# Second mixer: keys in columns with the meta keys as side columns, both kinds of values in one row stream

## The reference

```
hn   = rms_norm(h) * gain                    # h: 16 meta tokens and 256 tokens
proj = hn @ w_in                             # 1024 -> 1824 columns
c_q, c_kv, k_rope, dq, dk, dv, sq, sk, sv = split(proj)
#  256   128    32     256 256 256 384 128 128
y_a = mla(c_q, c_kv, k_rope)                 # 6 heads, through small second projections
y_b = differential(dq, dk, dv)               # 4 heads, two softmaxes each, 32 wide
y_c = sliding_window(sq, sk, sv, sinks)      # 6 heads, 2 key heads, 64 wide
h   = h + concat(y_a, y_b, y_c) @ w_out
```

## Time and profile before

| | us |
|---|---|
| median of 3 runs | 1275.91 (1275.83 to 1276.12) |
| the profiled execution | 1275.87, span 1274.0 |
| TensorE busy | 1264.8 (99%), granted clock 0.998 |
| VectorE busy | 1000.2 (79%) |
| ScalarE busy | 725.3 (57%) |
| POOL busy | 141.8 (11%) |
| chain that ended last | 98% TensorE |

### The profile page before, as it was taken

One profiled execution on the slowest core, in us unless ns is written; L12 is line 12 of the kernel. 1 busy time (PEld: TensorE's weight loads), 2 busy tenths in 40 slices (PEclk: granted clock), 3 DMA queues, 4 the chain that ended last, 5 costly groups with the idle time before them and its releaser, 6 DMA issues.

```text
span 1274.0 us, 24520 instructions
## 1 busy us (share of the span) xinstructions
PE 1264.8 (99%) x8467; PEld 1132.9 (89%) x8467; DVE 1000.2 (79%) x1873; ACT 725.3 (57%) x1337; POOL 141.8 (11%) x232
## 2 busy tenths in 40 slices
PE   9999999999999999999999999999999999999997
PEld 8999999898999999999999889999998878888886
DVE  7977778968887789777786758877777788877774
ACT  6655556765555566555565556555556756555553
POOL 5100004102430000000003202000004510000000
PEclk9999999999999999999999999999999999999999
DMA  9966655647996647666659637766666422766650
GB/s 286 287 188 192 183 181 157 156 126 210 266 273 185 191 136 229 188 193 182 184 148 258 186 100 224 225 185 191 186 177 153 154 70 83 222 190 183 192 168 33
DMA packets 294204, 233.31 MB, mean 183 GB/s; under 512 B 13244, under 2 KB 269572, under 8 KB 294144
## 3 DMA queue, kind: packets, MB, share of 16 engines
q1 hardware_dynamic: 287248, 213.87, 57.1%
q0 software_dynamic: 6720, 18.43, 5.6%
q10 hardware_dynamic: 176, 0.20, 0.0%
HBM read 229.53 MB, written 7.55 MB: 186 GB/s over the span
## 4 chain that ended last, share of the span: by engine, by line
PE 98%; ACT 0%; issue 0%; DVE 0%; POOL 0%; POOLq 0%; ACTq 0%
PE gu L2163 46%; PE y L2175 17%; PE y L2255 4%; PE gu L2547 4%; PE y L2217 3%; PE gu L2198 2%; PE gu L2371 2%; PE gu L2105 2%; PE gu L2340 2%; PE y L2198 2%; PE gu L2667 2%; PE gu L2562 1%; PE y L2585 1%; PE y L2574 1%; PE gu L2404 1%; PE gu L2631 1%
## 5 line engine op out<-in xcount | busy, mean ns | idle before, releaser
L2163 PE MATMUL gu<-sb_act_t,sb_w_hi 128*128 128x512 f32 x1664 | 582.1, 394 | 0.2 <-DVE sb_work L1575 0.2
L1424 DVE TENSOR_TENSOR sb_w_lo<-sb_w_raw,sb_w_hi 128x1024 fp32r<-128x1024 f32 x401 | 491.9, 1230 | 76.3 <-ACT sb_w_hi L954 70.5
L954 ACT ACTIVATE sb_w_hi<-sb_w_raw 128x1024 fp32r<-128x1024 f32 x401 | 418.4, 1049 | 27.5 <-PE y L2198 6.6
L2163 PE MATMUL gu<-sb_act_t,sb_w_lo 128*128 128x256 f32 x1664 | 430.5, 279 | 0.0
L2163 PEld LDWEIGHTS gu<-sb_act_t,sb_w_hi 128*128 128x128 f32 x1664 | 304.4, 188 | 54.9 <-issue 0.4
L2163 PEld LDWEIGHTS gu<-sb_act_t,sb_w_lo 128*128 128x128 f32 x1664 | 313.1, 188 | 14.7
L2175 PE MATMUL y<-sb_hid_t,sb_w_hi 128*128 128x256 f32 x1216 | 218.5, 280 | 0.0
L1036 ACT ACTIVATE sb_work<-gu 128x256 f32<-128x256 f32 x220 | 83.5, 381 | 203.2 <-PE gu L2163 198.7
L2175 PEld LDWEIGHTS y<-sb_hid_t,sb_w_hi 128*128 128x128 f32 x1216 | 191.0, 188 | 3.4
L2175 PE MATMUL y<-sb_hid_t,sb_w_lo 128*128 128x256 f32 x608 | 170.2, 280 | 0.0
L1575 DVE TENSOR_TENSOR sb_work<-gu,sb_work 128x256 f32<-128x256 f32 x220 | 92.5, 423 | 69.6 <-ACT sb_work L1036 69.6
(11 more groups left out here) (383 smaller groups left out, 1647.6 us busy)
## 6 DMA issues: line engine op xcount, KB each, us to landing
sb_w_raw<-in_ffn_w_down SPq DMA_DIRECT2D x88, 512.0 KB, 3.4
...
```

The costliest lines, as they stand in the source:

```text
L954: nc.scalar.activation(w_hi[:, slot, 0:w], w_raw[:, slot, 0:w], ACT.Copy).then_inc(hi_done, 1)
L1424: nc.vector.tensor_tensor(w_lo[:, slot, 0:w], w_raw[:, slot, 0:w], w_hi[:, slot, 0:w].bitcast(F32), ALU.subtract).then_inc(lo_done, 1)
L2163: ins = nc.tensor.matmul(gu[:, b, w, 0:width], part[:, s, cols], act_t[:, k, 0:width], start=(k == 0 and i == 0), stop=(k == KT - 1 and i ...
```

## The change

Keys are now made in columns, directly as `kt` wants them, and all values in one row stream:

- Row stream (first): 4 blocks of 2 x 384 columns, dv (256) and sv (128) side by side. A block is filled by two DMAs. The key row stream in j = 1 and 2 and all three sets of key transposes are gone, and with them the exchange, the adding and the scaling of those keys and ScalarE's copies to `kt`.
- `second_column_keys(i)`, new, three times (dk in two, sk in one): 24 matmuls each of 272 columns: 256 of the tokens and 16 of the meta tokens. For this the array `act_t` becomes `act_full`, 576 wide, with the meta tokens' hi part in 16 columns left of the tokens' hi part and their lo part in 16 columns right of the tokens' lo part. The hi x lo product writes its meta columns at the other end of the bank.
- `key_out(i)`, new, on VectorE: copies the 16 meta columns of one end, multiplies the 256 token columns by `row7`, and adds the 16 meta columns of the other end.
- `meta_to_hi` and `meta_to_lo` each have one more operation of 128 elements per partition, for these side columns.
- Blocks: 16 instead of 15. The order on TensorE is now: value stream, column keys 0 and 1, the scale rows, chunk 0, chunk 1, scores(0), latents; column keys 2 after the turn of j = 1; chunk 2 in j = 2 ahead of scores(3); chunk 3 after the turn of j = 2; nothing ahead of scores(4); chunk 4 after the turn of j = 3.

The core of the diff:

```
-IN2_BLOCKS = 15
-CHUNK_BLOCK = [4, 5, 12, 13, 14]
+IN2_DV, IN2_SV, IN2_V = 928, 1696, 384
+IN2_BLOCKS = 16
+CHUNK_BLOCK = [6, 7, 13, 14, 15]
+KEY_BLOCK = [4, 5, 12]
+LATENT_BLOCK = 8
+ACT_AT, META_HI, META_LO, ACT_W = 32, 16, 544, 576
...
-        act_t = sb("act_t", [P, KT, 2 * SEQ], F32R)
+        act_full = sb("act_t", [P, KT, ACT_W], F32R)
+        act_t = act_full[:, :, ACT_AT:ACT_AT + 2 * SEQ]
...
+        def chunk_bank(c):
+            return y[:, 2 + c, 0:SEQ] if c < 2 else gu[:, (c + 1) % 2, 1, 0:SEQ]
+        def column_keys(i):
+            return gu[:, i % 2, 1, :]
... (ScalarE)
+                nc.scalar.activation(act_full[:, :, META_HI:META_HI + META], src, ACT.Copy).then_inc(meta_hi, 1)
...
-                exchange(M_DK, 512, y[:, 1, :]).then_inc(meta_exchanged, 1)
+                exchange(M_DV, IN2_V, y[:, 1, 0:IN2_V]).then_inc(meta_exchanged, 1)
...
-                for c in range(2):
-                    act.wait_ge(k_turned, c + 1)
-                    nc.scalar.activation(kt[:, c, :], y[:, 2 + c, 0:KEYS2], ACT.Copy).then_inc(k_copied, 1)
...
-                    if j == 2:
-                        act.wait_ge(block_used, n0 + 12)
-                        exchange(M_SK, 256, gu[:, 0, 1, 0:256]).then_inc(meta_exchanged, 1)
-                        for t in range(TT):
-                            ins = nc.scalar.activation(wcol(t, S_SK, 256), gu[:, 1, 1, t * SEQ:(t + 1) * SEQ], ACT.Copy, scale=over_rms[t])
-                        ins.then_inc(proj_ready, 1)
-                    if j == 3:
-                        act.wait_ge(k_turned, 3)
-                        nc.scalar.activation(kt[:, 2, :], gu[:, 1, 1, 0:KEYS2], ACT.Copy).then_inc(k_copied, 1)
... (VectorE)
+            def key_out(i, n0):
+                dve.wait_ge(block_used, n0 + KEY_BLOCK[i] + 1)
+                bank = column_keys(i)
...
+                chain(nc.vector.tensor_copy(of_meta, bank[:, 0:META]))
+                nc.vector.tensor_tensor(of_tile, bank[:, META:META + SEQ].rearrange("p (t c) -> p t c", t=TT),
+                                        row7.rearrange("p (t c) -> p t c", t=TT), ALU.mult)
+                nc.vector.tensor_tensor(of_meta, bank[:, META + SEQ:META + SEQ + META], of_meta, ALU.add).then_inc(k_copied, 1)
...
                 dve.wait_ge(rows_copied, 1)
+                key_out(0, n0)
+                split(4)
+                key_out(1, n0)
+                split(5)
                 chunk_out(0, n0)
-                split(4)
-                split(5)
+                split(6)
                 chunk_out(1, n0)
-                split(6)
...
-                    if j in (1, 2):
-                        add_metas(j)
+                    if j == 1:
+                        add_metas(1)
+                    if j == 2:
+                        key_out(2, n0)
... (TensorE)
+            def second_column_keys(i, n0):
+                n = n0 + KEY_BLOCK[i]
+                s, bank = n % RING, column_keys(i)
+                pe.wait_ge(lo_done, n + 1)
+                if i == 2:
+                    pe.wait_ge(tile_out, 1)
+                    pe.wait_ge(meta_ready, 2)
+                for k in range(KT):
+                    cols = slice(k * P, (k + 1) * P)
+                    hi, lo = act_full[:, k, META_HI:ACT_AT + SEQ], act_full[:, k, ACT_AT + SEQ:META_LO + META]
+                    nc.tensor.matmul(bank[:, 0:KEYS2], w_hi[:, s, cols], hi, ...)
+                    nc.tensor.matmul(bank[:, META:META + KEYS2], w_hi[:, s, cols], lo, ...)
+                    ins = nc.tensor.matmul(bank[:, 0:KEYS2], w_lo[:, s, cols], hi, ...)
+                ins.then_inc(block_used, 1)
...
-                for q in second_rows(n0, 0, 4, 512, [(gu[:, 0, t, :], True) for t in range(TT)], [(y[0:MROWS, 1, :], True, 0)]):
+                for q in second_rows(n0, 0, 4, IN2_V, [(gu[:, t, 0, 0:IN2_V], True) for t in range(TT)], [(y[0:MROWS, 1, 0:IN2_V], True, 0)]):
                     pass
-                second_chunk(0, n0)
+                second_column_keys(0, n0)
+                second_column_keys(1, n0)
...
                 ins.then_inc(rows_made, 1)
-                pe.wait_ge(proj_ready, used + 1)
-                pe.wait_ge(meta_ready, 1)
-                for c in range(2):
-                    second_keys(y[:, 2 + c, :], S_DK + P * c, M_DK + P * c).then_inc(k_turned, 1)
+                second_chunk(0, n0)
                 second_chunk(1, n0)
                 second_scores(0)
...
                     if j == 2:
-                        next(keys)
-                    if j == 3:
...
-                        second_keys(gu[:, 1, 1, :], S_SK, M_SK).then_inc(k_turned, 1)
-                        second_chunk(3, n0)
+                        second_chunk(2, n0)
...
                     if j == 1:
-                        next(keys)
+                        second_column_keys(2, n0)
                     if j == 2:
-                        second_chunk(2, n0)
+                        second_chunk(3, n0)
```

More of the change, by code:

```diff
@@ L265, in width_of @@
     return SEQ if un.u < len(EVEN_U) + len(ODD_U) else SEEN[t]
-IN_HALVES = [FIRST[8] + CHUNK_BLOCK[c] for c in (2, 3)]
+IN_HALVES = [FIRST[8] + i for i in range(4)] + [FIRST[8] + CHUNK_BLOCK[c] for c in (2, 3)]
 PARTS = 4
@@ L286, in widths @@
     for kind, n in STEPS:
-        out += [2 * 416 if kind == "second" and 6 <= i < 10 else BLK for i in range(n)]
+        if kind == "second":
+            out += [2 * IN2_V] * 4 + [BLK] * (LATENT_BLOCK - 4) + [2 * 416] * 4 + [BLK] * (n - LATENT_BLOCK - 4)
+        else:
+            out += [BLK] * n
     return out
@@ L615, in _ @@
                             n += 1
-                        for k in range(0, KT, 4):
-                            load(n, n % RING, w_in_v[:, k:k + 4, IN2_SK:IN2_SK + 2 * P], (4, 2 * P))
-                            n += 1
+                        load(n, n % RING, w_in_v[:, :, IN2_SK:IN2_SK + P], (KT, P))
+                        n += 1
                         for h0, h1 in SWA_PAIRS:
@@ L1013, in meta_to_hi @@
                 for d in range(2):
[L1014 to L1015 removed]
+                    nc.scalar.activation(meta_v[:, :, d, d, :], src, ACT.Copy)
+                nc.scalar.activation(act_full[:, :, META_HI:META_HI + META], src, ACT.Copy).then_inc(meta_hi, 1)
             def final_norm():
@@ L1254, in second_mix @@
                     if j == 4:
-                        split(15)
+                        split(16)
                     if pair[0].diff:
@@ L2416, in second_scores @@
                 pair = SECOND_PAIRS[j]
+                if j == 0:
+                    pe.wait_ge(proj_ready, MIX["second"][4] + 1)
+                    pe.wait_ge(meta_ready, 1)
                 if j < 4:
-                    pe.wait_ge(k_copied, 2)
+                    pe.wait_ge(k_copied, 1 + j // 2)
                     pe.wait_ge(chunk_ready, 1 + j // 2)
@@ L2793, in second_mix @@
                 ins.then_inc(rows_made, 1)
[L2794 to L2797 removed]
+                second_chunk(0, n0)
                 second_chunk(1, n0)
                 second_scores(0)
[L2800 to L2803 removed]
+                latents = second_rows(n0, LATENT_BLOCK, 4, 416, [(gu[:, t, 1, 0:416], True) for t in range(TT)],
+                                      [(gu[0:MROWS, 0, 1, 416:512], False, 256), (gu[0:MROWS, 1, 1, 416:480], False, 352)], [(k_copied, 2)])
                 next(latents)
```

66 lines of the change are left out of this document (32 added, 34 removed).

## The result

The changed kernel takes 1282.26 us (median of 6 runs, 1280.09 to 1283.54) against 1276.01 before; the ratio is 1.0046 with a 95% interval of 1.0033 to 1.0059. It is slower by 6.2 us where I forecast no change. The runs scatter by 3.5 us, those of the kernel before by 0.4. The profiled execution is the slowest one, 1283.54 us with a span of 1281.7. One execution of e18 (2604 us) and one of the kernel before beside e17 and e18 (1768 us) stand far off all others and are left out of the medians here.

The account below looks back on a forecast made before the run. TensorE, busy for 99% of the span, was taken to bound the kernel. Work -3.7, column sums +2.0, later waits +2.7, old gaps -0.9 and first block's mixer +0.1 gave +0.2: 1275.87 to 1276.1 us, range 1273.2 to 1278.3.

Parts of the forecast that it names:

- TensorE's work: Second mixer: shorter value stream, no key row stream or key transposes, against added column-key matmuls; -3.7 us.
- Column sums: Within the value stream: TensorE arrives sooner and waits for POOL's last add of squares; +2.0 us.
- Chunk 3, turn and third latent step: After scores(0): new waits for the third key output, pair 2's probabilities and ScalarE's latent copy; 1.2 + 0.3 + 1.2 = +2.7 us.
- moves with scores(0): Chain to the third key output: ScalarE's and VectorE's halves of split(11) shift with scores(0), 3.5 us later.
- `key_out`: VectorE, between splits ahead of scores(0): each key output takes 0.75 us (0.5 to 1.0), covered by chunks 0 and 1.
- The first block's mixer: Added side-column operations stand ahead of a chain over the distance biases; +0.1 us (0 to 0.28).
- DMA "far from its limit in these stretches": Around the second mixer: DMA was taken to be far from its limit.
- Rival 3: Scores(0)'s 3.5 us delay carries whole to the latent copy: 1279.4 us, or 1277.7 with some idle gone; chance 0.13.
- where they stood before, within 0.2 us: Behind the third latent step: all engines stand as in the kernel before, within 0.2 us.

Follow-up runs that it names:

- e18: Changed kernel with late column sums, aligned tokens, maxima ahead of two splits, earlier third key output, and hidden tiles moved by 128 bytes; 1268.44 us.
- e17: Kernel before with 32 unused columns ahead of and 32 behind the hidden tiles, so only these move by 128 bytes; 1269.81 us.
- e11: As e10, but with the column sums where the change has them; 1278.82 us.
- e10: Changed kernel with column sums moved behind the value stream, tokens 256 bytes into their rows and the array's end padded by 256 bytes; 1276.05 us.
- e3: Kernel before with the column sums two k earlier, so that TensorE must wait for POOL's last add; 1282.13 us.
- e13: As e10, with VectorE's splits 10 and 12 behind the maxima of pairs 2 and 3 instead of ahead of them; 1274.14 us.
- e12: As e10, with TensorE's order changed to value stream, keys 0, chunk 0, scale rows, keys 1, scores(0), chunk 1; 1276.26 us.
- e1: Kernel before with only the tokens' array changed: 576 columns per k instead of 512, tokens from column 32 on; 1279.0 us.
- e4: Changed kernel with the column sums behind the value stream, after the second k of the first column keys; 1278.7 us.

## Why the prediction was wrong

- TensorE's work, -3.7 us: right in its unit prices, 0.175 measured against 0.1745 forecast at 384 columns and 0.125 against 0.127 at 272.
- Column sums, +2.0 us: the first step that failed. The wait was rightly named and 1.60 us long, but I counted a wait as its own length, and nothing for the clock behind it. TensorE ran at 1.2 GHz for up to 7 us there. In e11 against e10 the place costs 2.8 us in the median and 0.9 in an execution that kept its clock; in e3 3.4 us beyond the wait.
- Chunk 3, turn and third latent step, +2.7: 1.17, 0.25 and 1.23 us, that is 2.65. The chain was named rightly up to split 11; by e13 its removable part is the splits ahead of the maxima, by the rows split 10. That it moves with scores(0) was too loose: e12 moved scores(0) and the wait stayed, since the chain moves with the latents' end.
- `key_out`, 0.75: it took 0.71 (1010.66 to 1011.37 in e10).
- The first block's mixer, +0.1: not tried alone. In e10 and e11, which have its added operations and not the cost of the layout, the second mixer starts at 959.82 and 959.43, against 959.54. So it is under 0.3.
- Missing altogether, and the second step that failed: the change widens and shifts `act_t`, which the gate and up matmuls and the mixers' projections read. I had costed the array at nothing, without a sentence. By e1 it costs 2.9 us, by e4 against e10 2.7, by the changed kernel against e11 3.4.
- DMA "far from its limit in these stretches": that holds for the rows, but not between them, where the DMA share (ahead of the GB/s) is 0.95 and 1.11. From 980 on in the kernel before:

```profile
980.00:990.00 10.00, 10.00 (x78) 9.32 (x80) 7.89 (x23) 5.48 (x14) 1.61 (x3) 1.00 1.11 303
```

No wait of TensorE for a DMA shows in the second mixer, before or after.

The 6.2 us split into 1276.05 (e10) + 2.8 (e11 - e10) + 3.4 (the changed kernel - e11) = 1282.3. These are differences of one chain of runs, so they close whatever the terms are; what supports them is that e3 and e1 show the two effects by themselves in the kernel before.

The forecast of 1276.1 has its counterpart in e11's execution at full clock, 1276.9. It is not that near in its parts. Without the wait at the sums its terms give 1274.1, and e10, which is that kernel, takes 1276.05. The profile of e10 (1275.75) spreads the rest over the whole mixer: it starts 0.3 us late, and takes about 0.2 more than forecast up to scores(0), 0.4 up to chunk 3, 0.3 up to the latent step and 0.5 behind it, where I had all engines "where they stood before, within 0.2 us".

Rival 3 gave the right sign by a mechanism that did not act. In the changed kernel the latent step stands 7.1 us late: 3.3 are the start of the mixer and about 3.1 the clock. In e11, without these two, it stands 66.35 us behind the start of the mixer, against 65.68 in the kernel before: 0.7 later, where the rival has 3.5.

What stays open is why the places cost. No run shows the mechanism: only that the gate and up matmuls are faster with the tokens at 128 past 256 than at 0, that of the hidden tiles' three places tried 64 is the best for the down projections, and that the gate and up matmuls lose about 1 ns each when the hidden tiles leave 192, without reading them. X and work at 0 were not tried alone. Why an idle of 1.2 or 1.6 us costs the clock in some executions and not in others is open too.
